# Every fourth slot of two expert passes summed by VectorE in SBUF instead of TensorE in PSUM

## The chip, the cores and the metric

The kernel runs on one core of a Trainium2 chip. The metric is the device time of one execution in microseconds (us); the median of three runs is given, and one further execution was recorded by the hardware profiler.

## The reference, cut to what matters

The reference is a network of three blocks over 256 tokens of width 1024, all in fp32. The last two blocks each end in a PEER layer, a mixture of single-neuron experts. For every token 8 heads choose 16 of 16384 experts each, so 128 experts per token, and

```
h   = sum_d x[t, d] * u[expert, d]          # one dot product per token and expert
a   = gelu(h) * gate
out = sum over the 128 experts of a * v[expert, :]
x   = layer_norm(ALPHA * x + out)
```

`u` and `v` are tables of 16384 rows of 1024 numbers. The rows that are chosen differ from token to token, so they have to be gathered from memory: 8 KB (`u` row and `v` row) per token and expert.

## The kernel before, in words

**Passes and slots.** The 256 tokens are two tiles of 128 (one token per SBUF partition). The two PEER layers and the two tiles make four passes (`PASSES`: layer 0 tile 0, layer 0 tile 1, layer 1 tile 0, layer 1 tile 1), which I number 0 to 3. A pass has 128 slots; slot n (0 to 511 over all passes) handles one expert of each of the 128 tokens of a tile. What the kernel calls the second and third pass are passes 1 and 2, slots 128 to 383.

**One slot.** POOL (GpSimd) waits until a gather buffer is free, then issues an indirect DMA (L2254) that brings 128 rows of 8 KB, 1 MB in all, into one of six buffers (`gbuf`, `GBUF = 6`, used in turn). DVE (VectorE) waits for the landing and computes the dot product with one instruction over 128x1024 (`dot`, L2544) into one column of `hdot`. ACT (ScalarE) applies gelu to that column (L2082), makes a 128x128 diagonal of the gates (L2076, `gate_diagonal`, one slot ahead) and multiplies it by the column (L2089, `diag`, five buffers). PE (TensorE) multiplies this diagonal by the `v` half of the buffer, in two halves of 512 columns, and adds into two PSUM banks which hold the pass's sum (`add_slot`, L1456). The second half's instruction raises `buffer_free`, for which POOL waits six slots later (`wait_freed`).

**What runs beside it.** Slots are only the beat. Four tables (`pe_steps`, `act_steps`, `dve_steps`, and `routing_parts` within the last) say which other work is done ahead of which slot's work on each engine; each engine runs its list strictly in order. In pass 0 that is the queries, keys and routing of the two tiles of layer 0. In passes 1 and 2 it is the whole of the second block for one tile each: keys and values, queries, six dilated-attention units, memory attention, output product, layer norm, and then the PEER queries (16 blocks, `peer_q`, at 96 to 132 slots after the pass's start) and keys. The routing on DVE (top 16 by repeated max, index and one-hot steps) falls into slots 107 to 180 counted from the pass's start, so its later part lies in the next pass. ACT and DVE do their share of a step `LATER = 3` slots or more after PE's. At three slots into the next pass DVE closes the pass before (`add_to_x`, L2547: x = ALPHA*x + sum from PSUM, then statistics) and three slots later normalises (`layer_norm`, L2364).

**Weights.** SP streams weight slots of 128x1024 fp32, in pairs of 1 MB, through a ring of eight slots (L1677) as PE gives them back. The sequence for passes 1 and 2 is laid down in `weight_slots` (`layer`, 44 slots for each of the two tiles). The 16 query blocks of the last PEER layer are partly kept in SBUF: `KEPT` names the even-numbered ones, eight blocks that are loaded once and used in both passes; the other eight go through the ring twice. Four kept blocks have a place of their own, four lie in the arena at columns 0 to 4095.

**Kept loads.** POOL loads the first four kept blocks early, three more after the intra-chunk part of the gated attention of the second block (L2222 to L2224), and the last, which lies at arena column 0, after the last output of that attention has been computed (L2238), just before the first gather. The POOL queue is in order, so the head weights of the first two PEER heads (L2231) come between.

Of the kernel before, what the change touches and what calls it, by code (L numbers as in the profile page):

```python
# [13 lines left out]
ALU = mybir.AluOpType  # L14
ACT = mybir.ActivationFunctionType
AX = mybir.AxisListType.X

P = 128
# [6 lines left out]
PAIR = 2  # L25
KEPT = tuple(range(0, 16, 2))
NEG = -1e30
# [121 lines left out]
def add(table, slot, name, *what):  # L149

    table.setdefault(slot, []).append((name, what))


# [348 lines left out]
def weight_slots(a):  # L502
# [53 lines left out]
    out += [np.zeros((P, SLOT), np.float32)] * (len(out) % PAIR)  # L556
    out += [last_q[i] for i in KEPT]
    out += peer_q[:4] + slots_of_columns(bw[:, 2304:]) + slots_of_rows(a["w_out_2"][1])[NK - 2:]
# [69 lines left out]
def build(nc, x_in, memT_in, weights, consts, where, rows_in, peer_uv, out):  # L628
# [5 lines left out]
    with ctx:  # L634
# [15 lines left out]
        rows = sb("row_ring", [P, NROW, D])  # L650
        kept_apart = sb("kept_queries", [P, len(KEPT) // 2, SLOT])
        cst = sb("const_tile", [P, n_const])
# [142 lines left out]

        kept_queries = [kept_apart[:, i, :] for i in range(4)] + [area(SLOT * i, SLOT) for i in (1, 2, 3, 0)]
        gbuf = [area(4 * SLOT + 2 * D * b, 2, D) for b in GATHER_PLACES]
# [101 lines left out]
        def _(pe):  # L899
# [550 lines left out]
            def add_slot(n):  # L1450

                pe.wait_ge(sem("diag_ready"), n + 1)
                for h in range(2):
# [240 lines left out]
        def _(act):  # L1694
# [383 lines left out]
            def weighted(n):  # L2078

                s = n % P  # L2080
                act.wait_ge(sem("dotted"), n + 1)
                done(act.activation(hdot[:, s:s + 1], hdot[:, s:s + 1], ACT.Gelu), "peer_gelu")  # L2082
                if n + 1 < SLOTS:
                    gate_diagonal(n + 1)
                if n >= DIAGS:
                    wait_freed(act, n - DIAGS)
                act.wait_ge(sem("gate_diag"), n + 1)
                act.wait_ge(sem("peer_gelu"), n + 1)
                done(act.activation(diag[n % DIAGS], gate_diag[n % 2], ACT.Copy, scale=hdot[:, s:s + 1]), "diag_ready")  # L2089
# [98 lines left out]
        def _(pool):  # L2188
# [30 lines left out]
            for r in range(NROW, SPREAD):  # L2219
                if r == NROW + 3:  # L2220
                    wait_drained(pool, ("gla_intra", 0))
                    pool.dma_start(kept_w, weights[n_slots - 2, :, :]).then_inc(sem("kept_loaded"), 16)  # L2222
                    for i in range(4, len(KEPT) - 1):
                        load_kept(i)  # L2224
                pool.wait_ge(sem("rows_used"), r - NROW + 1)
                load_row(pool, r)
                if r == 7:
# [7 lines left out]
                    for i, m in enumerate((mem_k, mem_v)):  # L2235
                        pool.dma_start(kept_out[1][i], last[:, 1024 + 512 * i:1536 + 512 * i]).then_inc(sem("kept_out_loaded"), 16)
            wait_filled(pool, ("gla_o", 3))
            load_kept(len(KEPT) - 1)  # L2238
            for n in range(SLOTS):
# [11 lines left out]
                if n >= GBUF:  # L2251
                    wait_freed(pool, n - GBUF)
                pool.sem_inc(sem("gather_turn"), 1)
                pool.indirect_dma_start(gbuf[n % GBUF].rearrange("p a d -> p (a d)"), None, peer_uv,  # L2254
# [4 lines left out]
        def _(dve):  # L2259
# [279 lines left out]
            def dot(n):  # L2539
# [4 lines left out]
                dve.scalar_tensor_tensor(u, u, 1.0, x[:, t, :], ALU.mult, ALU.mult, accum_out=hdot[:, s:s + 1])\  # L2544
                    .then_inc(sem("dotted"), 1)

            def add_to_x(stage_name, t):  # L2547
# [465 lines left out]
            for n in range(SLOTS + 2 * LATER + 1):  # L3013
                for name, what in DVE_STEPS.get(n, []):
# [14 lines left out]
                    if name == "close":  # L3029
                        p, = what  # L3030
                        if p < len(PASSES) - 1:
                            add_to_x(f"sum{p}", PASSES[p][1])
# [25 lines left out]
                    if name == "out_norm":  # L3058
                        layer_norm(3 + 2 * what[0], what[0], 8, 9, "x_ready")
                if n < SLOTS:  # L3060
                    dot(n)


# [33 lines left out]
```

## Time and profile before

| | |
|---|---|
| median of 3 runs | 2069.1 us (2067.74 to 2071.44) |
| the profiled execution | 2072.72 us |
| its span, first to last instruction | 2070.9 us |
| PE busy | 1895.9 us, 92% of the span |
| DVE busy | 1382.5 us, 67% |
| ACT busy | 896.6 us, 43% |
| POOL busy | 616.1 us, 30% |
| DMA | 708.06 MB, mean 342 GB/s |
| first gather issued, last gather issued | 627.0 us, 2049.8 us |

Busy time is the union of an engine's instructions; idle time is attributed to the instruction that ended it. GB/s counts the bytes of all DMA packets that started in a stretch. The four passes, by the start of their first dot product, begin at 638, 985, 1361 and 1739 us; the last dot product starts at 2059.7 us.

### The profile page before, as it was taken

The page shows a single profiled execution, that of the slowest core. Times are in us where ns is not written, and L with a number is a line of the kernel's source. Part 1 is how long each engine was busy: PE and PEld are TensorE (multiplying, and loading weights), DVE is VectorE, ACT ScalarE, POOL GpSimd, SP SyncE. Part 2 cuts the span into 40 slices and gives each one's busy share as a digit, 9 for nine tenths or more (in the row PEclk, how much of TensorE's full clock was granted, in tenths as well). Part 3 has the DMA queues.
Part 4 walks back from the last instruction along what each step waited for, and adds up shares of the span by engine and source line. Part 5 has one row for each costly group of instructions (what it writes and reads, how often), then busy time and mean ns, then how long its engine had stood idle before and what let it go on. Part 6 is the DMA issues. An engine that isn't in the chain of part 4 may idle for free. (4 is left out here: it accounts for less than half of the span.)

```text
span 2070.9 us, 24820 instructions
## 1 busy us (share of the span) xinstructions
PE 1895.9 (92%) x8012; PEld 1169.3 (56%) x8012; DVE 1382.5 (67%) x2957; ACT 896.6 (43%) x2417; POOL 616.1 (30%) x567
## 2 busy tenths in 40 slices
PE   8999999999998999988899998999999899877776
PEld 8788668887955654433456544556664355322222
DVE  8778666666738677776665545766865575985444
ACT  5657454444534333333334533343455334343332
POOL 0002200000003344444333334443334434444442
PEclk9999999999999999999999999999999999999999
DMA  6623555554658999999999999999999999999997
GB/s 253 224 108 123 194 184 192 193 183 152 235 186 354 390 421 419 418 418 414 400 421 421 421 419 410 417 422 421 417 414 391 416 416 387 422 421 419 421 419 317
DMA packets 99373, 708.06 MB, mean 342 GB/s; under 512 B 11040, under 2 KB 11184, under 8 KB 14896
## 3 DMA queue, kind: packets, MB, share of 16 engines
q0 software_dynamic: 77504, 552.25, 65.1%
q1 hardware_dynamic: 21600, 154.15, 19.8%
q8 instruction: 64, 1.05, 0.2%
q14 instruction: 61, 0.50, 0.1%
q10 hardware_dynamic: 144, 0.11, 0.0%
HBM read 705.42 MB, written 1.05 MB: 341 GB/s over the span
## 5 line engine op out<-in xcount | busy, mean ns | idle before, releaser
L1456 PE MATMUL bank<-arena 128*128 128x512 f32 x2048 | 980.6, 609 | 145.4 <-ACT arena L2089 142.1
L2544 DVE SCALAR_TENSOR_TENSOR arena<-arena,x_tok 128x1024 f32<-128x1024 f32 x512 | 627.1, 1226 | 466.7 <-DMA arena<-peer_uv,arena 461.1
L2254 POOL DMA_INDIRECT arena<-peer_uv,arena x512 | 580.9, 1135 | 850.1 <-PE bank L1456 649.4
L1456 PEld LDWEIGHTS bank<-arena 128*128 128x128 f32 x2048 | 362.0, 191 | 639.4 <-ACT arena L2089 339.7
L2082 ACT ACTIVATE arena<-arena 128x1 f32<-128x1 f32 x512 | 103.6, 202 | 841.7 <-DVE arena L2544 837.7
L2089 ACT ACTIVATE arena<-arena 128x128 f32<-128x128 f32 x512 | 197.7, 386 | 0.5
L2076 ACT ACTIVATE arena<-const_tile,arena 128x128 f32<-128x128 f32 x512 | 197.8, 386 | 0.0
L925 PEld LDWEIGHTS bank<-xT,weight_ring 128*128 128x128 f32 x1248 | 165.5, 191 | 37.0 <-issue 31.1
L925 PE MATMUL bank<-xT,weight_ring 128*128 128x128 f32 (+1 forms) x1248 | 177.2, 294 | 0.9 <-DVE xT L2281 0.9
L925 PE MATMUL bank<-x_low_high,z_high 128*128 128x512 f32 (+1 forms) x480 | 135.8, 351 | 1.5 <-issue 1.5
L1201 PE MATMUL bank<-x_split,w_split 128*128 128x512 f32 x704 | 129.0, 342 | 2.6 <-DVE x_split L2824 2.6
L1201 PEld LDWEIGHTS bank<-x_split,w_split 128*128 128x128 f32 x704 | 110.4, 190 | 20.0 <-issue 2.8
L2806 DVE TENSOR_TENSOR w_split<-weight_ring,w_split 128x1024 fp32r<-128x1024 f32 x66 | 80.8, 1225 | 36.9 <-ACT w_split L1917 36.2
L925 PE MATMUL bank<-x_low_high,ring_low 128*128 128x256 f32 x368 | 104.0, 283 | 0.0
L925 PEld LDWEIGHTS bank<-x_low_high,z_high 128*128 128x128 f32 x480 | 83.5, 190 | 17.1 <-issue 5.2
L871 POOL DMA_DIRECT2D row_ring<-rows_in x8 | 4.5, 571 | 286.6 <-DVEq L2354 200.4
L1917 ACT ACTIVATE w_split<-weight_ring 128x1024 fp32r<-128x1024 f32 x66 | 69.7, 1060 | 42.7 <-PE bank L1201 26.6
L1704 ACT ACTIVATE arena<-bank 128x512 f32<-128x512 f32 (+6 forms) x143 | 67.7, 498 | 45.0 <-PE bank L925 38.1
L925 PE MATMUL bank<-arena 128*64 128x128 f32 (+10 forms) x664 | 74.7, 311 | 2.5 <-DVE arena L2304 1.8
L925 PEld LDWEIGHTS bank<-x_low_high,ring_low 128*128 128x128 f32 x368 | 70.5, 192 | 0.0
L925 PEld LDWEIGHTS bank<-arena 64*128 64x128 f32 (+6 forms) x664 | 54.4, 169 | 28.1 <-issue 23.6
L1767 ACT ACTIVATE z_high<-weight_ring 128x1024 fp32r<-128x1024 f32 x50 | 51.8, 1053 | 34.3 <-PE bank L925 25.5
(322 smaller groups left out, 2035.7 us busy)
## 6 DMA issues: line engine op xcount, KB each, us to landing
weight_ring<-weights SPq DMA_DIRECT2D x145, 1024.0 KB
arena<-peer_uv,arena POOLq DMA_INDIRECT x512
arena<-weights POOLq DMA_DIRECT2D x9, 512.0 KB, 7.9
row_ring<-rows_in POOLq DMA_DIRECT2D x8, 512.0 KB, 4.7
kept_queries<-weights POOLq DMA_DIRECT2D x4, 512.0 KB, 9.8
const_tile<-consts POOLq DMA_DIRECT2D x1, 1657.0 KB, 8.9
x_tok<-x_in SPq DMA_DIRECT2D x2, 512.0 KB, 4.9
memT<-memT_in POOLq DMA_DIRECT2D x1, 1024.0 KB, 7.5
```

Of the source, the lines that this page charges most:

```text
L925: ins = pe.matmul(o, lhsT, rhs, start=start, stop=stop, is_transpose=turn or None)
L1201: ins = pe.matmul(o, lhsT, rhs, start=start, stop=stop)
L1456: ins = pe.matmul(b[:, :], diag[n % DIAGS], gbuf[n % GBUF][:, 1, h * 512:(h + 1) * 512], start=n % P == 0, stop=n % P == P - 1)
L1704: done(act.activation(o, i, f, **kw), "drained_by_act" if last else "act_step")
L1767: done(act.activation(z_high[:, i % SPLITS, :], ring[:, slot % RING, :], ACT.Copy, scale=scale), "z_high")
L1917: done(act.activation(w_split[n % SPLITS][:, 0, :], ring[:, slot % RING, :], ACT.Copy), "slot_high")
L2076: done(act.activation(gate_diag[n % 2], ident, ACT.Copy, scale=w[:, s:s + 1]), "gate_diag")
L2082: done(act.activation(hdot[:, s:s + 1], hdot[:, s:s + 1], ACT.Gelu), "peer_gelu")
L2089: done(act.activation(diag[n % DIAGS], gate_diag[n % 2], ACT.Copy, scale=hdot[:, s:s + 1]), "diag_ready")
L2254: pool.indirect_dma_start(gbuf[n % GBUF].rearrange("p a d -> p (a d)"), None, peer_uv, bass.IndirectOffsetOnAxis(ap=expert[t][:, s:s + 1]. ...
L2544: dve.scalar_tensor_tensor(u, u, 1.0, x[:, t, :], ALU.mult, ALU.mult, accum_out=hdot[:, s:s + 1])\
L2806: done(dve.tensor_tensor(w[:, 1, :], ring[:, slot % RING, :], w[:, 0, :], ALU.subtract), name)
```

## The change

In passes 1 and 2, from the eighth slot of the pass on, every slot with n % 4 == 2 (30 per pass, 60 in all) is not summed by PE. DVE adds `hdot * v` into an SBUF tile `summed` (128x1024, arena column 0) with one instruction, right behind the dot product of the next slot, and frees the buffer itself. For these slots ACT makes no diagonals; it multiplies the 128x1 gelu column by the gate column in place. The pass's close adds `ALPHA * x` to `summed` and then the PSUM halves. `summed` is cleared once per pass. Its place was that of the eighth kept query block, so seven are kept (0, 2, ..., 12), block 14 goes through the ring in both passes, and kept blocks 4 to 6 are loaded behind the head weights.

```diff
-KEPT = tuple(range(0, 16, 2))
+KEPT = tuple(range(0, 14, 2))
...
+def by_dve(n):
+    return P <= n < 3 * P and n % P >= 8 and n % 4 == 2
+
+def gate_no(n):
+    return sum(not by_dve(i) for i in range(n + 1))
...
-    out += [last_q[i] for i in KEPT]
+    out += [last_q[i] for i in KEPT] + [np.zeros((P, SLOT), np.float32)] * (len(KEPT) % PAIR)
...
+        summed = area(0, SLOT)
...
             def add_slot(n):                                   # PE
+                if by_dve(n):
+                    return
...
             def weighted(n):                                   # ACT
...
-                if n + 1 < SLOTS:
+                if n + 1 < SLOTS and not by_dve(n + 1):
                     gate_diagonal(n + 1)
+                if by_dve(n):
+                    w = gate_w[slot_of(n)[1]].rearrange("p h k -> p (h k)")
+                    act.wait_ge(sem("peer_gelu"), n + 1)
+                    done(act.activation(hdot[:, s:s + 1], hdot[:, s:s + 1], ACT.Copy, scale=w[:, s:s + 1]), "diag_ready")
+                    return
...
-                act.wait_ge(sem("gate_diag"), n + 1)
+                act.wait_ge(sem("gate_diag"), gate_no(n))
...
                     pool.dma_start(kept_w, weights[n_slots - 2, :, :]).then_inc(sem("kept_loaded"), 16)
-                    for i in range(4, len(KEPT) - 1):
-                        load_kept(i)
...
-            wait_filled(pool, ("gla_o", 3))
-            load_kept(len(KEPT) - 1)
+            for i in range(4, min(len(KEPT), 7)):
+                load_kept(i)
...
+            def add_slot(n):                                   # DVE
+                s = n % P
+                if n % P > 10:
+                    wait_freed(dve, n - 4)
+                dve.wait_ge(sem("diag_ready"), n + 1)
+                dve.scalar_tensor_tensor(summed, gbuf[n % GBUF][:, 1, :], hdot[:, s:s + 1], summed, ALU.mult, ALU.add)\
+                    .then_inc(sem(f"buffer_free{n % GBUF}"), 1)
+
+            def add_summed(p):
+                t = PASSES[p][1]
+                wait_freed(dve, P * (p + 1) - 2)
+                step(dve.scalar_tensor_tensor(summed, x[:, t, :], ALPHA, summed, ALU.mult, ALU.add))
+                for h in range(2):
+                    cols = slice(h * 512, (h + 1) * 512)
+                    wait_filled(dve, (f"sum{p}", h))
+                    done(dve.tensor_tensor(x[:, t, cols], summed[:, cols], bank((f"sum{p}", h))[:, :], ALU.add), "drained_by_dve")
+                settle()
+                statistics(t)
...
-                        if p < len(PASSES) - 1:
+                        if p in (1, 2):
+                            add_summed(p)
+                        elif p < len(PASSES) - 1:
                             add_to_x(f"sum{p}", PASSES[p][1])
...
+                if n in (P + LATER + 4, 2 * P + LATER + 4):
+                    step(dve.memset(summed, 0.0))
                 if n < SLOTS:
                     dot(n)
+                if by_dve(n - 1):
+                    add_slot(n - 1)
```

## Rows read from the trace of the kernel before

**Rows 1.** The page, part 2: 40 slices of 51.8 us.
```profile
DMA  6623555554658999999999999999999999999997
GB/s 253 224 108 123 194 184 192 193 183 152 235 186 354 390 421 419 418 418 414 400 421 421 421 419 410 417 422 421 417 414 391 416 416 387 422 421 419 421 419 317
```

**Rows 2.** Windows: stretch, length, busy us (x) of PE, PEld, DVE, ACT, POOL, clock, DMA.
```profile
638.00:985.00 347.00, 309.38 (x931) 159.94 (x930) 252.34 (x657) 136.77 (x443) 146.96 (x129) 0.99 1.01 414
985.00:1361.00 376.00, 347.21 (x1383) 198.57 (x1382) 228.08 (x515) 151.94 (x463) 143.84 (x129) 0.99 1.01 416
1361.00:1739.00 378.00, 359.33 (x1510) 215.12 (x1509) 248.36 (x586) 160.07 (x473) 146.94 (x128) 1.00 1.01 411
1739.00:2060.00 321.00, 258.06 (x579) 94.99 (x578) 207.40 (x461) 112.99 (x397) 138.54 (x125) 1.00 1.00 415
...
1900.00:1950.00 50.00, 39.95 (x82) 13.69 (x81) 24.95 (x41) 15.72 (x60) 20.75 (x21) 1.00 1.01 422
```

**Rows 3.** Timeline of bare slots in pass 0: start us, duration us, engine, line.
```profile
981.27 0.20 ACT L2082 ACTIVATE arena<-arena 128x1 f32<-128x1 f32 x1 [1.69 <-DVE arena L2544]
...
981.67 0.39 ACT L2089 ACTIVATE arena<-arena 128x128 f32<-128x128 f32 x1
982.11 1.98 PE L1456 MATMUL bank<-arena 128*128 128x512 f32 x4 [0.49 <-ACT arena L2089]
982.49 1.23 DVE L2544 SCALAR_TENSOR_TENSOR arena<-arena,x_tok 128x1024 f32<-128x1024 f32 x1 [1.26 <-DMA arena<-peer_uv,arena]
982.74 1.79 POOL L2254 DMA_INDIRECT arena<-peer_uv,arena  x1 [1.87 <-issue]
...
984.91 0.94 POOL L2254 DMA_INDIRECT arena<-peer_uv,arena  x1 [0.39 <-issue]
```

**Rows 4.** The page, part 6: DMA issues of SP for the weight ring.
```profile
weight_ring<-weights SPq DMA_DIRECT2D x145, 1024.0 KB
```

**Rows 5.** Windows of stretches in passes 1 to 3, columns as in rows 2.
```profile
1300.00:1330.00 30.00, 25.95 (x111) 14.78 (x110) 27.70 (x86) 11.75 (x36) 10.32 (x11) 1.00 1.01 421
...
1380.00:1400.00 20.00, 18.41 (x80) 10.97 (x80) 17.71 (x57) 8.12 (x28) 9.39 (x8) 1.00 1.02 422
1470.00:1490.00 20.00, 19.07 (x91) 12.35 (x90) 18.46 (x60) 8.85 (x24) 6.80 (x7) 1.00 1.01 418
...
1520.00:1590.00 70.00, 68.25 (x314) 42.93 (x315) 40.92 (x79) 40.19 (x107) 28.27 (x25) 1.00 0.99 393
...
1680.00:1700.00 20.00, 19.42 (x85) 11.50 (x84) 18.71 (x67) 7.34 (x26) 8.47 (x8) 1.00 1.01 419
1700.00:1730.00 30.00, 30.00 (x143) 19.16 (x143) 19.77 (x37) 13.20 (x40) 12.17 (x12) 1.00 0.99 375
1740.00:1760.00 20.00, 18.93 (x79) 10.90 (x78) 14.50 (x24) 9.86 (x29) 8.93 (x8) 1.00 1.00 390
```

**Rows 6.** Chain of waits: by line in 1696 to 1765 us; one piece, start and length.
```profile
by line: PE bank L1456 56.3%; PE bank L925 28.5%; DMA arena<-peer_uv,arena 14.8%; issue 3.2%; DVE arena L2544 1.8%; POOL arena L2254 1.4%; ACT arena L2089 0.6%; ACT arena L2082 0.3%; ACT arena L2076 0.1%; POOLq L2253 0.0%
...
1646.83 5.15 PE bank L1456 x12
...
2029.93 10.00 DMA arena<-peer_uv,arena
```

**Rows 7.** The first gather alone: POOL's timeline, then windows, columns as in rows 2.
```profile
560.07 1.57 POOL L2211 DMA_DIRECT2D arena<-weights  x3
...
626.98 1.02 POOL L2254 DMA_INDIRECT arena<-peer_uv,arena  x1 [7.22 <-DVE arena L2474]
...
604.00:610.00 6.00, 6.00 (x15) 2.46 (x13) 1.75 (x4) 0.29 (x1) 0.00 (x0) 1.00 0.00 0
...
629.00:631.00 2.00, 2.00 (x6) 0.81 (x5) 1.79 (x8) 0.00 (x0) 0.00 (x0) 1.00 0.87 307
```

**Rows 8.** One line of DVE in 985 to 1739 us: busy us, mean ns, idle before.
```profile
L2369 DVE SCALAR_TENSOR_TENSOR x_tok<-x_tok,arena,row_ring 128x1024 f32<-128x1024 f32 x4 | 5.1, 1284 | 0.1
```

**Rows 9.** Window with a lower granted clock, columns as in rows 2.
```profile
1460.00:1470.00 10.00, 8.03 (x24) 4.36 (x23) 7.02 (x13) 5.58 (x14) 4.06 (x4) 0.83 1.02 422
```

More of the change, by code:

```diff
@@ L650, in build @@
         rows = sb("row_ring", [P, NROW, D])
-        kept_apart = sb("kept_queries", [P, len(KEPT) // 2, SLOT])
+        kept_apart = sb("kept_queries", [P, 4, SLOT])
         cst = sb("const_tile", [P, n_const])
@@ L794, in build @@
         mem_PT = [area(25552 + 512 * b, 4, P) for b in range(2)]
-        kept_queries = [kept_apart[:, i, :] for i in range(4)] + [area(SLOT * i, SLOT) for i in (1, 2, 3, 0)]
+        kept_queries = [kept_apart[:, i, :] for i in range(4)] + [area(SLOT * i, SLOT) for i in (1, 2, 3)]
+        summed = area(0, SLOT)
         gbuf = [area(4 * SLOT + 2 * D * b, 2, D) for b in GATHER_PLACES]
@@ L2252, in _ @@
                     wait_freed(pool, n - GBUF)
+                if n == 2 * P // 4 and len(KEPT) == 8:
+                    load_kept(7)
                 pool.sem_inc(sem("gather_turn"), 1)
```

## The prediction

> **What bounds the kernel now.** I read the page's slices first. From 627 us on, where the gathers begin, the DMA engines stand at 9 in every slice but the last and move 387 to 422 GB/s, with three exceptions at the start [rows 1]. The reader is to see a ceiling: the best slices all end at 421 or 422. The windows of the four passes come next [rows 2]. In 1900:1950, where nothing runs but gathers, the rate is 422 GB/s while PE is busy 40 of 50 us and DVE 25 of 50: neither holds the gathers back. So the transfer of bytes is the bound, and an engine matters only where it keeps the rate under 422. What could be won at most is the shortfall, (422 - rate)/422 of each stretch: pass 1 376 x 6/422 = 5.3 us, pass 2 378 x 11/422 = 9.9 us. PE is busy 347 of 376 us and 359 of 378 us there, and that looks like the bound but is not by itself; a busy PE under a full DMA costs nothing.
>
> Where the shortfall lies [rows 5]: 1520:1590 has 70 x 29/422 = 4.8 us, with PE 68 of 70 us and DVE only 41; 1700:1730 has 30 x 47/422 = 3.3 us, with PE 30 of 30 us; 1740:1760, at the close of pass 2, has 1.5 us. The chain of waits agrees for 1696 to 1765: PE 85%, DVE 2% [rows 6]. In pass 1 the shortfall is scattered and stands mostly at layer norms, where DVE is the cause.
>
> How an engine comes to cost DMA time: there are six buffers. A gather issued under load takes 10.0 us to land [rows 6], of which most is queueing, since a lone one, issued at 626.98, moves at 307 GB/s in 629:631 and so needs about 5 us for its 1 MB [rows 7]. Some 5 us of delay in freeing a buffer are thus swallowed by a shorter queue before the DMA runs dry. In a bare slot the buffer is free about 4.1 us after its landing: dot 1.23, gelu and diagonals 0.2 + 0.39 + 0.39, matmuls 1.98, with the hand-overs [rows 3].
>
> **The change part by part.**
>
> *Bytes.* Sixteen query blocks less seven kept leave nine per pass in the ring instead of eight: two weight slots more, one pair of 1 MB. 145 pairs [rows 4] become 146. At 422 GB/s that is 1.05 MB / 0.422 = 2.5 us, inside the stretch that the DMA bounds, and nothing hides it: **+2.5 us**. The load of the eighth block, which goes away, ran just before the first gather, in a stretch with DMA to spare, and gives nothing back.
>
> *Kept loads moved.* Three loads go from 560 us to behind the head weights, about 594 to 596 us. POOL issues them in 1.57 us [rows 7] and then waits until 627 for the first expert anyway. They need 1.5 MB / 0.42 = 3.7 us of DMA, and 604:610 moves nothing at all, so they are done long before 627. They are queued behind the head loads, so they delay neither these nor (SP issues none until 611) the ring. At 560 they no longer compete with the ring; PE was waiting little there. I take -0.3 us, bounds -1.0 and +0.5.
>
> *PE.* 60 slots less. Their four matmul parts take 1.98 us alone and 5.15 / 3 = 1.72 us in a row [rows 3, 6]: 60 x 1.72 = 103 us of PE less, 52 per pass. That is worth only what it adds to the DMA rate. In 1520:1590 about 24 gathers pass, six of them by DVE: 10.3 us of PE's 68.25 go, leaving 58 of 70. I take 4.0 of the 4.8 us, bounds 0 and 4.8. In 1700:1730 PE loses 3 x 1.72 = 5.2 of 30 us, but DVE comes in with a backlog (next part), so I take 1.5 of 3.3 us. Sum **-5.5 us**.
>
> *ACT.* Two diagonals of 0.39 us become one 128x1 instruction of 0.2 us [rows 3]. ACT is busy 152 and 160 us per pass [rows 2], so nothing changes. The new wait of DVE for ACT: the column of slot n is ready some 0.6 us behind its dot product, and DVE asks for it after the next one, 2.5 us later. Behind the waiting instruction on DVE stand the routing and softmax steps and the next dot. Only where ACT itself is late, waiting for PE, does it hold; with PE unloaded I take 0 and keep +1.
>
> *DVE.* The add reads two 128x1024 tensors and writes one. The nearest rows are L2544 with 1.23 us [rows 3] and L2369 with 1.28 us [rows 8]; I take 1.28. 60 x 1.28 = 77 us, on 228 + 248 us busy in 754 [rows 2]: from 63% to 73%. Harmless on average, not in the peaks where routing and attention meet. Adding 1.28 us for each such slot to the busy time [rows 5]: 1300:1330 27.7 + 4 x 1.28 = 32.8 of 30, over by 2.8; 1470:1490 18.5 + 2.6 = 21.0 of 20, over by 1.0; 1680:1700 18.7 + 2.6 = 21.3 of 20, and it goes on into 1700:1710, together up to 3.3 over; 1380:1400, with the longer close, 17.7 + 2.6 + 1.3 = 21.5 of 20, over by 1.5. What is over becomes a later dot and a later free buffer, against some 5 us of slack of which PE's lag, now shorter, had used a part. Also the buffer of such a slot is no longer held by PE at all: freed two DVE instructions after the next landing, 2.5 + 1.23 + 1.28 = 5.0 us instead of 4.1, less where PE lags. I take +1.0 us for the peaks, bounds 0 and 8.6.
>
> *Closes and clearing.* The two halves from PSUM stay, and one instruction over 128x1024 of 1.28 us [rows 8] comes ahead of them, twice. Dots of the next pass wait behind it. At 1380:1400 the rate is 422, so there is slack; at 1740:1760 there is none (390). The two clears of 128x1024 have no row; by the same 1.28 us each they are 2.6 us of DVE at most, in a slot that has room. I take +1.2 us in all, bounds 0 and 5.
>
> *PE's clock.* In passes 1 and 2 bare stretches now leave PE idle some 3 us behind every fourth slot. In 1460:1470 PE was idle 2 of 10 us and the granted clock was 0.83, so a third of the stretch ran at the lower level of 1.2 GHz; the DMA rate stayed at 422 [rows 9]. Such falls may come more often, but in the bare stretches, where the queue has its 5 us of slack. I take 0, bound +2.
>
> Sum: 2.5 - 0.3 - 5.5 + 1.0 + 1.2 = -1.1 us. The profiled execution took 2072.7 us, of which 2070.9 is the span and 1.8 lies around it; it stands 3.6 us above the median of the runs. The change of -1.1 us is put on the median: 2069.1 - 1.1 = **2068.0 us**. Differences below 0.2%, 4.1 us, cannot be told from no change, so the forecast is no change.
>
> *A rule against it.* A gather's issue on POOL takes 0.94 us, but the one at 982.74, begun while DVE's two-input dot of 982.49 ran, took 1.79 [rows 3]. The Trainium skill (SBUF — State Buffer, section "SBUF: two separate sides") states that DVE instructions of this kind and GpSimd share one port pair, and that the loser blocks until the other has finished. By that rule, with which this row agrees, each of the 60 added instructions is another such holder, and the sum would gain what rival C works out from rows; by the average of the rows, in which POOL idles more than half of the time, it gains nothing, and that is what I take.
>
> **The rivals.**
>
> *A, PE's relief comes through whole (faster).* For: in the shortfalls PE is full and the chain is PE's. Against: 1300:1330 and 1680:1700 show DVE at 92 to 94%. All of the shortfall in 1520:1590 and 1700:1730 goes, 8.1 us, and the DVE terms are nil: 2069.1 + 2.5 - 0.3 - 8.1 = 2063.2 us.
>
> *B, DVE takes PE's place (slower).* Place: the four peaks and the two closes. It decides once a dot starts over 5 us behind its landing. For: DVE is over 100% in each of them by the sums above; in 1700:1730 the rate is already low while the DVE backlog of 1680:1700 is worked off. Against: each lasts only 20 to 30 us. Price: peaks 8.6, closes 1.5 + 1.3, PE's relief only 4.0 since 1700:1730 becomes DVE's: 2069.1 + 2.5 - 0.3 + 8.6 + 2.8 - 4.0 = 2078.7 us in full; with half of the peaks and closes 2073.0. I put it at 2076.
>
> *C, POOL's issue is held by the adds (slower).* At most 1.79 - 0.94 = 0.85 us for each. With slack it costs nothing; in the 120 us of 1520:1590, 1700:1730 and 1740:1760, 10 adds x 0.85 = 8.5 us at the most; with half of it on top of the forecast 2072, and where it also meets the DVE backlog 2074.
>
> *D, the relief is where PE was not the bound.* Then nothing of -5.5 comes and 2069.1 + 2.5 - 0.3 + 2.2 = 2073.5 us: barely slower.
>
> **How the numbers follow.** The forecast of no change 0.47 (its own range 2065 to 2073), A 0.22, B 0.20, C 0.04, D 0.07. Faster by over 0.2% is A: 0.22. Slower by over 0.2% is B, C and D: 0.31. The rest is 0.47. The range runs from A's time to B's value: 2063 to 2076.5; below it is only a wholly hidden pair of weights, above it DVE peaks paid in full.
>
> **What would show it.** 146 ring pairs. PE's busy time down by about 100 us, DVE's up by about 80 us. The rate in 1520:1590 (at that place of pass 2) at 415 or more, not 393: the step for PE. A rate of about 375 still behind 1700, with DVE full: B. Rates under 415 in the places of 1300:1330 and 1470:1490: B too. POOL's mean issue time well above its present one: C. The pass lengths 376 and 378 us should become about 378 and 375. The forecast is wrong if either differs by over 4 us, or if the first gather is not issued within 1 us of 627.

## The result, and the profile after

The changed kernel takes 2080.8 us (median of six runs, 2077.6 to 2084.3); the kernel before took 2069.5 us in the six runs beside them. The ratio is 1.0046, interval 1.0032 to 1.0061: slower by 0.46%, or 9.5 us. (The two medians differ by 11.3 us, which the interval holds too; the ratio is the figure used below.) The forecast was 2068.0 us and no change, with 2076.5 us as the upper end of the range. Both missed it. Of the cases it comes nearest to B, DVE in PE's place (2078.7 us in full), though not by B's own sum, as the last part shows.

In the ratios below, 0.001 is 2.07 us. The profiled execution took 2079.8 us, the span 2078.0 us of it.

The page of the kernel after: span, engines, and the 40 slices, here of 52 us. They answer to [rows 1].

```profile
span 2078.0 us, 24346 instructions
PE 1825.7 (88%) x7772; PEld 1136.3 (55%) x7772; DVE 1458.4 (70%) x3021; ACT 882.0 (42%) x2357; POOL 620.8 (30%) x566
DMA  6633555545549999999999999999999999999997
GB/s 239 223 139 105 203 197 196 185 162 183 203 183 383 407 421 421 421 417 413 413 421 419 407 422 400 395 421 422 420 394 414 397 394 393 416 421 421 421 414 314
```

The reader sees the same ceiling of 421 to 422 GB/s as before. PE's busy time is 1825.7 us, 70 us less, and DVE's 1458.4 us, 76 us more (before: 1895.9 and 1382.5 us). The windows of the four passes answer to [rows 2]; columns as there.

```profile
633.00:980.00 347.00, 310.20 (x936) 160.44 (x936) 252.22 (x659) 137.19 (x443) 148.64 (x128) 0.99 1.01 414
980.00:1359.00 379.00, 310.44 (x1252) 181.21 (x1252) 264.17 (x545) 143.17 (x433) 145.22 (x127) 0.95 1.00 412
1359.00:1745.00 386.00, 328.67 (x1422) 202.53 (x1421) 287.33 (x620) 152.46 (x444) 149.49 (x129) 0.96 1.00 407
1745.00:2066.00 321.00, 255.81 (x552) 92.63 (x550) 208.22 (x461) 112.88 (x397) 138.88 (x124) 0.99 1.00 415
```

Pass 1 is 3 us longer (379 against 376), pass 2 is 8 us longer (386 against 378); the passes that the change leaves alone stand. Worked out as in the prediction, (422 - rate)/422 of each pass, the two lose 9.0 and 13.7 us to rates under 422, 22.7 us together, where before they lost 15.2 us. These 7.5 us more and 2.5 us for the new pair's bytes make 10.0 us: apart from the pair's bytes, the loss is time in which the DMA ran below its ceiling. DVE has 264 and 287 us in them, where it had 228 and 248. Then the ring's row, the added instruction, and the matmuls, which answer to [rows 4] and to PE's rows in [rows 3]:

```profile
weight_ring<-weights SPq DMA_DIRECT2D x146, 1024.0 KB
L2571 DVE SCALAR_TENSOR_TENSOR arena<-arena 128x1024 f32<-128x1024 f32 x60 | 76.8, 1281 | 0.0
L1469 PE MATMUL bank<-arena 128*128 128x512 f32 x1808 | 899.8, 628 | 225.6 <-ACT arena L2107 222.6
```

The add takes 1281 ns, sixty times: 76.8 us, as forecast from [rows 8]. The 146 pairs are there. PE is 70 us less busy and not 103: the rest is the lower clock, by which one matmul now takes 628 ns in the mean and took 609, which over 1808 of them is 34 us (the granted clock over the span is 0.977 and was 0.991). The trace has 16 falls to the lower level in passes 1 and 2, 75 us in all, where before had 3 and 14 us. PE had been idle between slots ahead of them: in the two passes it has 26 pauses of over 2 us, up to 4.8 us, where before it had 2.

The places of [rows 5], moved by the few us by which the passes moved:

```profile
1298.00:1328.00 30.00, 20.85 (x96) 12.53 (x94) 29.21 (x84) 10.19 (x32) 10.63 (x10) 1.00 1.01 416
1380.00:1400.00 20.00, 18.15 (x77) 10.62 (x76) 17.17 (x53) 7.17 (x24) 8.17 (x8) 1.00 1.02 421
1473.00:1493.00 20.00, 17.15 (x96) 12.16 (x95) 18.23 (x59) 7.64 (x19) 6.58 (x7) 1.00 1.01 421
1523.00:1593.00 70.00, 61.68 (x293) 39.37 (x292) 47.30 (x83) 37.29 (x95) 29.16 (x26) 0.98 1.01 412
1687.00:1707.00 20.00, 14.18 (x67) 8.76 (x66) 19.48 (x65) 4.54 (x18) 8.32 (x7) 1.00 0.96 385
1707.00:1737.00 30.00, 26.61 (x125) 16.72 (x124) 23.17 (x40) 13.13 (x40) 12.87 (x13) 1.00 0.96 366
1746.00:1766.00 20.00, 16.36 (x58) 8.77 (x57) 16.32 (x26) 9.97 (x29) 7.49 (x7) 0.91 0.99 402
```

DVE is full in the first (29.2 of 30 us) and the fifth (19.5 of 20), and the rates are 416 (was 421), 385 (419) and 366 (375). 1380:1400 and 1473:1493 keep 421. 1523:1593 rose from 393 to 412, which looked like PE's relief; the experiments do not bear that out. What DVE does ahead of the 366 is in its timeline, with a gather's issue at the end:

```profile
1700.99 1.22 DVE L2562 SCALAR_TENSOR_TENSOR arena<-arena,x_tok 128x1024 f32<-128x1024 f32 x1
1702.14 1.28 DVE L2571 SCALAR_TENSOR_TENSOR arena<-arena 128x1024 f32<-128x1024 f32 x1
1703.34 0.75 DVE L2432 MAX8 arena<-arena 128x8 f32<-128x256 f32 x2
1704.12 1.22 DVE L2562 SCALAR_TENSOR_TENSOR arena<-arena,x_tok 128x1024 f32<-128x1024 f32 x1
1704.23 1.93 POOL L2272 DMA_INDIRECT arena<-peer_uv,arena  x1 [3.11 <-DVE arena L2571]
```

Dot, add, top-8 step and dot follow each other without a gap: here DVE does not wait for a landing, and POOL's gather of 1704.23 has waited 3.11 us for the add L2571 to free its buffer. The chain of waits over 1674 to 1745 us, against [rows 6] where PE had 85% and DVE 2%:

```profile
by line: DMA arena<-peer_uv,arena 42.8%; DVE arena L2562 16.2%; issue 13.1%; PE bank L1469 5.6%; DVE arena L2571 4.1%; DVE arena L2430 2.8%; DVE arena L2434 2.8%; POOL arena L2272 2.7%; DVE arena L2428 2.6%; DVE arena L2432 2.1%; DVE arena 
```

PE's matmuls of the sum are down to 5.6%; the named lines of DVE make 30.6%, and the gathers' flights (from issue to landing) 42.8%.

### The profile page after: what moved, and what is told of

The parts are those of the page before. It is cut to its first block and busy times, and to the rows that moved or that the text cites. A ratio compares the mean times of both kernels' runs of the same rounds, so it can differ in the third digit from the quotient of the medians.

```text
span 2078.0 us, 24346 instructions
## 1 busy us (share of the span) xinstructions
PE 1825.7 (88%) x7772; PEld 1136.3 (55%) x7772; DVE 1458.4 (70%) x3021; ACT 882.0 (42%) x2357; POOL 620.8 (30%) x566
## 5 line engine op out<-in xcount | busy, mean ns | idle before, releaser
L1469 PE MATMUL bank<-arena 128*128 128x512 f32 x1808 | 899.8, 628 | 225.6 <-ACT arena L2107 222.6
L2272 POOL DMA_INDIRECT arena<-peer_uv,arena x512 | 586.2, 1145 | 879.6 <-PE bank L1469 577.8
L1469 PEld LDWEIGHTS bank<-arena 128*128 128x128 f32 x1808 | 325.6, 195 | 688.9 <-ACT arena L2107 424.1
L936 PEld LDWEIGHTS bank<-xT,weight_ring 128*128 128x128 f32 x1280 | 171.1, 194 | 33.7 <-issue 27.2
L936 PE MATMUL bank<-xT,weight_ring 128*128 128x128 f32 (+1 forms) x1280 | 183.5, 297 | 0.8 <-DVE xT L2299 0.8
L2107 ACT ACTIVATE arena<-arena 128x128 f32<-128x128 f32 x452 | 176.5, 390 | 7.5
L2089 ACT ACTIVATE arena<-const_tile,arena 128x128 f32<-128x128 f32 x452 | 175.5, 388 | 0.0
L1930 ACT ACTIVATE w_split<-weight_ring 128x1024 fp32r<-128x1024 f32 x66 | 69.8, 1062 | 42.5 <-PE bank L1212 26.6
L2571 DVE SCALAR_TENSOR_TENSOR arena<-arena 128x1024 f32<-128x1024 f32 x60 | 76.8, 1281 | 0.0
L936 PE MATMUL bank<-weight_ring,arena 128*128 128x512 f32 (+1 forms) x192 | 64.9, 528 | 0.2 <-ACT arena L1717 0.2
```

The source lines that it names most:

```text
L936: ins = pe.matmul(o, lhsT, rhs, start=start, stop=stop, is_transpose=turn or None)
L1469: ins = pe.matmul(b[:, :], diag[n % DIAGS], gbuf[n % GBUF][:, 1, h * 512:(h + 1) * 512], start=n % P == 0, stop=n % P == P - 1)
L1930: done(act.activation(w_split[n % SPLITS][:, 0, :], ring[:, slot % RING, :], ACT.Copy), "slot_high")
L2089: done(act.activation(gate_diag[n % 2], ident, ACT.Copy, scale=w[:, s:s + 1]), "gate_diag")
L2571: dve.scalar_tensor_tensor(summed, gbuf[n % GBUF][:, 1, :], hdot[:, s:s + 1], summed, ALU.mult, ALU.add)\
```

## The experiments

All ratios are to the kernel before, with 95% intervals; they reach 0.1 to 0.15% to either side, so the difference of two ratios is known to 0.15 or 0.2%, 3 to 4 us. The diffs are cut and against the changed kernel, except that of e2. Three kernels form the base: e1 has the bytes without the adds, e3 the bytes and DVE's time without the adds' relief, e4 the relief without DVE's time.

**e1, no adds.** Seven blocks kept, loads moved, no sum by DVE.

```diff
 def by_dve(n):
-    return P <= n < 3 * P and n % P >= 8 and n % 4 == 2
+    return False
...
-                        if p in (1, 2):
-                            add_summed(p)
-                        elif p < len(PASSES) - 1:
+                        if p < len(PASSES) - 1:
...
-                if n in (P + LATER + 4, 2 * P + LATER + 4):
-                    step(dve.memset(summed, 0.0))
```

> All of the change but the sums: seven kept query blocks, block 14 through the ring twice, kept loads 4 to 6 behind the head weights; PE sums every slot as before. Theory 1 (VectorE's peaks, and the lower TensorE clock that its adds leave behind, make the loss): only the bytes remain, 2.5 us, less what the moved loads give (the profile of the changed kernel issued its first gather 4.4 us earlier): 2067 to 2072 us, passes 1 and 2 as long as before plus 2.5 us together. Rival (the extra ring pair costs more than its bytes because PE waits for it): 2075 us or more, with PE waiting for weight_ring in passes 1 and 2.

Measured: 1.0011 [1.0001, 1.0020], 2072.2 us. That is +2.3 us for the pair of 1 MB, where the prediction had 2.5 - 0.3. The interval runs from 0.2 to 4.1 us, and e5 and e8 below, with the same bytes, measured 1.0000; so the size of this term is known to some 2 us only.

**e2, the kernel before with the kept loads moved alone.**

```diff
-                    for i in range(4, len(KEPT) - 1):
-                        load_kept(i)
...
+            for i in range(4, len(KEPT) - 1):
+                load_kept(i)
             wait_filled(pool, ("gla_o", 3))
```

> The kernel before with kept loads 4 to 6 issued behind the head weights and nothing else; eight kept. If the 4.4 us that the changed kernel's profile gained ahead of the first gather come from this step, it reads 2065 us and a first gather at 622 to 623 us. If they are the spread of one profile against another (the change's own forecast was -0.3 us), it reads 2069 us and the first gather stands anywhere from 622 to 628.

Measured: 0.9998 [0.9990, 1.0007]. The move is worth nothing that can be told.

**e3, DVE's time alone.** e1 with the clears and sixty instructions of the add's form, whose result nobody reads.

```diff
-                if by_dve(n - 1):
-                    add_slot(n - 1)
+                if P < n <= 3 * P and (n - 1) % P >= 8 and (n - 1) % 4 == 2:
...
+                    dve.scalar_tensor_tensor(summed, x[:, slot_of(n - 1)[1], :], 1.0, summed, ALU.mult, ALU.add)\
+                        .then_inc(sem("filler"), 1)
```

> e1 with 60 instructions of 128x1024 more on VectorE at the places of the adds, and two clears, which no other engine needs and whose result is not used; PE sums every slot, so its lag and its clock stay those of before. Theory 1a (VectorE's peaks alone): shortfall of the DMA rate rises at the four places of the changed kernel's (slots 112 to 119 of pass 1, 40 to 55, 88 to 95 and 112 to 119 of pass 2) by some 10 us or more, since PE's lag is not relieved: 2080 us or more. Theory 1b (the clock of a PE that idles is the larger part): under 2075 us.

Measured: 1.0045 [1.0029, 1.0060], 2079.1 us. The whole loss is there, with PE doing all 128 slots of a pass: 0.34% or 7.0 us above e1, by the two intervals 3 to 11 us. One of these idle instructions (idle in that they do nothing for the result) took 1223 ns:

```profile
L3108 DVE SCALAR_TENSOR_TENSOR arena<-x_tok,arena 128x1024 f32<-128x1024 f32 x60 | 73.4, 1223 | 0.0
```

**e4, PE's relief alone.** The sixty slots are left out of the sum, ACT frees their buffers, DVE adds nothing; the clears and the longer closes are out too.

```diff
                     done(act.activation(hdot[:, s:s + 1], hdot[:, s:s + 1], ACT.Copy, scale=w[:, s:s + 1]), "diag_ready")
+                    act.sem_inc(sem(f"buffer_free{n % GBUF}"), 1)
                     return
...
-                if by_dve(n - 1):
-                    add_slot(n - 1)
```

> The changed kernel without VectorE's adds, clears and the longer close: the 60 slots are left out of the sum altogether, ScalarE frees their buffers as soon as the gated column is ready. VectorE carries no more than before; PE has the changed kernel's gaps and clock. Theory 1a: PE's relief comes through, 8 us of shortfall go, 2.5 us of bytes come: 2062 to 2066 us in spite of falls of the clock. Theory 1b: the falls of the clock (16 in passes 1 and 2 against 3) eat the relief: 2069 us or more, with shortfall in bare slots 64 to 71 and behind layer norms.

Measured: 1.0008 [0.9998, 1.0018], 2071.6 us: 0.6 us under e1, which the intervals can't tell from nothing; 5.5 us less is outside them. It has 18 falls of the clock.

**e8, the relief given back as useless work.** e4, and for each slot left out PE multiplies zeros into the same banks.

```diff
                 if by_dve(n):
+                    pe.wait_ge(sem("diag_ready"), n + 1)
+                    for h in range(2):
+                        pe.matmul(bank((f"sum{n // P}", h))[:, :], c("eps")[:, 3:4].to_broadcast([P, P]), cst[:, where["keysT"][0]:where["keysT"][1]], start=False, stop=False)
                     return
```

> e4 with two matmuls of a zero column over constants on PE in the place and at the time of each sum left out (they add zero and hold no buffer): 103 us of PE work given back that does nothing. Theory 1b: falls of the clock go from 18 in passes 1 and 2 to 3, and the time is the same as e4's 2071.6 within 1.5 us, since what the idle saves the lower clock takes. Rival (relief in e4 was worth something and something else ate it): 2074 us or more.

Measured: 1.0000 [0.9990, 1.0010]. PE's busy time in the two passes is back (708 us; e1 705, e4 641), its clock falls 3 times as before the change, and the time is the same or less. The 103 us of matmuls have no price that can be told in this kernel, with them or without.

**e11, the same in the change itself.** The zero matmuls of e8 put into the changed kernel.

```diff
                 if by_dve(n):
+                    pe.wait_ge(sem("diag_ready"), n + 1)
+                    for h in range(2):
...
                     return
```

> The changed kernel whole, with e8's two zero matmuls on PE in place of each of the 60 sums: PE has the work and the clock of before, VectorE its adds. Theory (the relief of PE is worth nothing, since the clock takes it): 2079 to 2081 us, no slower than the changed kernel, about 3 falls of the clock in passes 1 and 2. Rival (relief is worth something against VectorE's backlog): 2083 us or more.

Measured: 1.0052 [1.0039, 1.0064], 2081.5 us, against 1.0046 of the change: what PE was relieved of is worth nothing measurable there either. The clock's falls are down to 5 in it (0.991 over the span), so they are not the cause of the loss.

The three places of the trace say the same. First the windows of e1, then of e3 and e4, at 1520:1590, at the end of pass 1, and at the end of pass 2; columns as before.

```profile
1520.00:1590.00 70.00, 68.01 (x315) 42.67 (x314) 41.04 (x80) 39.50 (x103) 28.08 (x25) 1.00 1.00 403
1320.00:1345.00 25.00, 22.82 (x102) 13.76 (x102) 16.95 (x35) 10.85 (x32) 11.03 (x9) 1.00 1.00 411
1695.00:1740.00 45.00, 44.84 (x205) 28.02 (x204) 29.78 (x66) 19.21 (x62) 17.94 (x17) 1.00 1.00 387
```

```profile
1520.00:1590.00 70.00, 69.57 (x327) 44.56 (x327) 50.68 (x96) 42.71 (x106) 27.46 (x24) 1.00 1.01 408
1320.00:1345.00 25.00, 22.07 (x97) 13.05 (x96) 23.20 (x48) 11.53 (x35) 9.02 (x9) 1.00 0.98 390
1695.00:1740.00 45.00, 41.29 (x179) 24.52 (x179) 38.50 (x92) 17.04 (x55) 17.03 (x16) 1.00 0.96 365
```

```profile
1520.00:1590.00 70.00, 60.86 (x275) 37.59 (x274) 40.58 (x79) 37.26 (x95) 23.95 (x24) 0.93 0.97 396
1320.00:1345.00 25.00, 20.12 (x99) 12.98 (x97) 13.57 (x26) 7.60 (x28) 10.37 (x11) 1.00 1.00 402
1695.00:1740.00 45.00, 41.41 (x204) 27.32 (x204) 30.16 (x61) 17.43 (x56) 21.54 (x18) 0.96 0.97 385
```

and of the kernel after and of e8:

```profile
1520.00:1590.00 70.00, 63.26 (x297) 40.03 (x295) 47.97 (x87) 38.97 (x100) 29.27 (x25) 0.98 1.01 411
1320.00:1345.00 25.00, 20.77 (x96) 12.87 (x95) 17.62 (x33) 10.09 (x29) 12.73 (x9) 1.00 0.94 366
1695.00:1740.00 45.00, 38.26 (x186) 24.48 (x185) 36.02 (x73) 17.09 (x54) 18.93 (x17) 1.00 0.95 370
```

```profile
1520.00:1590.00 70.00, 69.78 (x320) 43.47 (x318) 42.16 (x81) 37.52 (x97) 25.93 (x26) 1.00 1.00 411
```

At 1520:1590 the rate does not follow PE: 408 and 411 GB/s with PE at 69.6 and 69.8 of 70 us (e3, e8), 396 with PE at 60.9 (e4). The rise from 393 to 412 was no proof of the relief. (The windows stand at fixed times, and the slots in them shift by up to 6 us from profile to profile, so a few GB/s mean nothing.) At the other two places it goes with DVE: 390 and 365 with DVE at 23.2 of 25 and 38.5 of 45 us (e3), 366 and 370 in the kernel after, but 411 and 387 in e1, and 402 and 385 in e4, whose PE has 3.4 us less in the last. In the kernel after, DVE is busy only 17.6 of 25 us in the first of the two, but 29.2 of 30 us just ahead of it (1298:1328). The shortfall that e1 and the kernel before have in 1695:1740 (387 and 389) stays in e4, so PE's sums do not explain that one either; what does is open.

**e5, e6, e7: a few slots where PE was full.** e5 is e4 with 14 slots of pass 2 left out, 40 to 79 and 112 to 127. e6 has these summed by DVE. e7 has ten, 52 to 79 and 116 to 127, summed by DVE.

```diff
-    return P <= n < 3 * P and n % P >= 8 and n % 4 == 2
+    return (296 <= n < 336 or 368 <= n < 384) and n % 4 == 2
```

> e4 with only 14 of the 60 slots left out of the sum (slots 40 to 79 and 112 to 127 of pass 2, each fourth), where PE is full; buffers freed by ScalarE. Theory 1b (in e4 the falls of the clock ate the relief): few falls are added, the shortfall of pass 2 at slots 56 to 71 and 112 to 127 goes from some 6 us to 2: 2067 to 2069 us, 3 to 5 us under e1. Rival (PE was not what held the rate there): 2072 us, as e1.

> The change with only those 14 slots summed by VectorE; pass 1 closes as before. Theory (loss = VectorE's added time at its peaks, relief real where PE is full): most of the 7 us that VectorE's adds cost are gone, relief of 3 us stays, 1.3 us for the longer close: 2070 to 2072 us. Rival (a VectorE add costs the same wherever it stands): e1 plus 14/60 of 7 us = 2074 us.

> As e6 with the slots that lie in VectorE's two peaks taken out: 10 slots (52 to 79 and 116 to 127 of pass 2). Theory: 1 to 2 us under e6, 2069 to 2071 us, no slower than the kernel before. Rival: no different from e6.

Measured: e5 1.0000 [0.9990, 1.0009], e6 1.0007 [0.9997, 1.0018], e7 1.0011 [1.0000, 1.0021]. None is faster than the kernel before, and all three intervals overlap that of e1: e5 stands 0.11% under e1, which may be relief or nothing, and e6 and e7 can't be told from e5. Three of e7's ten slots (54, 118 and 122) lie in what e9 and e10 below count as DVE's full stretches.

**e9, e10: where DVE's time costs.** The idle instructions of e3, split: e10 has the twenty that fall in DVE's full stretches, e9 the other forty. The stretches are slots 88 to 95 (the layer norms) and 106 to 122 of both passes and 34 to 54 of pass 2.

```diff
+def peak(n):
+    return 216 <= n < 224 or 234 <= n <= 250 or 290 <= n <= 310 or 344 <= n < 352 or 362 <= n <= 378
...
+                loads = [i for i in range(P, 3 * P) if i % P >= 8 and i % 4 == 2 and not peak(i)]
+                if n - 1 in loads:
```

> e3 with 40 of its 60 idle VectorE instructions, those outside the stretches where VectorE is full (taken out: slots 88 to 95 and 106 to 122 of pass 1, 34 to 54, 88 to 95 and 106 to 122 of pass 2; 20 instructions). Theory (VectorE's added time costs only at its peaks): 2072.5 us, within 1.5 us of e1; e3's other 5 to 6 us of the 7 stand in the 20. Rival (each add costs the same): 2/3 of e3's 0.34%, 2077 us.

> The other 20 of e3's 60 instructions alone, those in the full stretches. Theory: 2077 to 2079 us, nearly e3. Rival (each costs the same): 1/3 of 0.34%, 2074.5 us.

Measured: e9 1.0011 [0.9999, 1.0022], nothing above e1. e10 1.0028 [1.0018, 1.0037], 0.17% above e1: a third of the instructions, half of the cost at the middle of the intervals. If each instruction cost the same wherever it stands, e9 would be at 1.0034, outside its interval; e10's own expectation, 2077 to 2079 us, was missed with 2075.8 us. The two together are 0.17% above e1 and e3 is 0.34%. The intervals are too wide to say whether the rest appears only with all sixty.

**e12, e18, e17: the same split with the real adds.** e12 sums the forty off the peaks by DVE, e18 the twenty in them; e17 is e12 with the zero matmuls of e8.

```diff
-    return P <= n < 3 * P and n % P >= 8 and n % 4 == 2
+    return P <= n < 3 * P and n % P >= 8 and n % 4 == 2 and not peak(n)
```

> The changed kernel with VectorE's sums at the 40 slots outside the full stretches only, the other 20 by PE. Theory: e1's 2072 us plus the longer closes, 1 to 2 us: 2073 to 2074 us, 7 us under the changed kernel. It does not beat the kernel before, whose bytes are fewer. Rival (each add costs the same): 2078 us.

> The changed kernel with VectorE's sums at the 20 slots in the full stretches only; PE's idle slots are fewer than in e12, in stretches where PE is full too. Theory (VectorE's time in its peaks costs 0.17% beside e1, and PE's relief there offsets part of it): 1.0015 to 1.0028, 2074 us. Rival (relief of PE is worth nothing and its idle slots cost as in e12): 1.003 or more.

> e12 with the two zero matmuls on PE in place of each of the 40 sums: the same adds, buffers and closes, PE's work and clock as before the change. Theory L (VectorE's work off the peaks costs only together with a PE that idles, whose clock falls): 1.0011 to 1.0018, 2072 to 2074 us, few falls. Rival (a real add costs whatever PE does): as e12, 1.0034, 2077 to 2078 us.

Measured: e12 1.0034 [1.0022, 1.0045], e18 1.0030 [1.0018, 1.0042], e17 1.0032 [1.0020, 1.0045]. e18 agrees with e10. e12 does not agree with e9: it is 0.23% above, and e17 shows that neither PE's idle time nor its clock is why. Nor is it a wait for ACT: the rows of the adds in e12 and e17 have 0.0 us of idle time before them. The theory set down for e12 (2073 to 2074 us) failed, and its rival, each add costs the same (2078 us), has the measured 2077.9; for e18 too the rival's 1.003 or more came. Forty adds cost 0.23% above e1, twenty 0.19%, sixty 0.35%: for the real adds a price per add fits within the intervals, and a price in the peaks alone does not. Windows of e12 and e18 at the two ends of passes:

```profile
1320.00:1345.00 25.00, 23.34 (x96) 13.63 (x96) 15.55 (x30) 10.57 (x32) 11.49 (x10) 1.00 1.01 415
1695.00:1740.00 45.00, 44.83 (x203) 27.85 (x204) 30.31 (x66) 18.14 (x58) 19.16 (x17) 1.00 0.99 389
```

```profile
1320.00:1345.00 25.00, 21.25 (x93) 13.23 (x93) 18.30 (x34) 10.50 (x32) 11.12 (x9) 0.93 0.93 377
1695.00:1740.00 45.00, 39.19 (x189) 25.12 (x188) 34.50 (x69) 17.42 (x56) 19.64 (x17) 1.00 0.96 371
```

The low rates at the peaks go with the adds in them (377 and 371 GB/s in e18, 415 and 389 in e12). What e12 loses lies elsewhere, scattered, and stays open.

The traces of all kernels show the same split in the dots themselves. I counted, over passes 1 and 2, how far a dot starts behind its landing, that is behind the last update of the semaphore for which it waits. It is over 4.5 us behind in five slots of the kernel after, 116 of pass 1 and 113 to 116 of pass 2; in the last four it grows 5.1, 5.2, 6.0, 6.5 us. The eight kernels with DVE's additional work in all of the peaks (the kernel after, e3, e10, e11, e14, e15, e16, e18) have 5 or 6 such slots each, all of them from 111 to 117 of pass 2 and at 115 or 116 of pass 1, with a largest lag of 6.5 to 7.4 us. The other twelve, e9, e12 and e17 among them (and e6 and e7, which have adds in some slots of the peaks), have none; their largest lag is 3.3 to 4.4 us. So the late dots go with the peaks' part of the loss, and they are not what e12 and e17 lose.

**e13, e14: the closes.** e13 is e1 with the change's clears and longer closes. e14 is the changed kernel with the close of before, so that DVE's sum is left out of x.

```diff
-    return P <= n < 3 * P and n % P >= 8 and n % 4 == 2
+    return False
...
-                wait_freed(dve, P * (p + 1) - 2)
```

> e1 with the clears of the sum tile and the longer closes of passes 1 and 2 alone; no slot is summed by VectorE. Theory H (the held buffer is what a real add costs): the closes are worth 1 to 2 us, 1.0011 becomes at most 1.0020, 2072 to 2074.5 us. Rival K (the closes are it): 4 us or more, 1.003 or more.

```diff
-                        if p in (1, 2):
-                            add_summed(p)
-                        elif p < len(PASSES) - 1:
+                        if p < len(PASSES) - 1:
```

> The changed kernel with the closes of before: what VectorE has summed in the 60 slots is left out of x. Theory H: 1 to 2 us under the changed kernel, 2079 us, 1.004. Rival K: 4 us or more under it, 1.0025 or less.

Measured: e13 1.0008 [0.9996, 1.0020], e14 1.0059 [1.0042, 1.0075]. The longer close costs nothing that can be told where it is added and gives nothing where it is taken away.

**e15, the buffers freed early.** e4 with the clears and the sixty idle instructions: DVE's time as in the change, but ACT frees the buffers.

```diff
+                if by_dve(n - 1):
+                    dve.wait_ge(sem("filler"), sum(by_dve(i) for i in range(n - 1)))
+                    dve.scalar_tensor_tensor(summed, x[:, slot_of(n - 1)[1], :], 1.0, summed, ALU.mult, ALU.add)\
+                        .then_inc(sem("filler"), 1)
```

> e4 (60 slots left out of the sum, buffers freed by ScalarE) with e3's 60 idle instructions on VectorE and its two clears: the changed kernel's load on VectorE and relief of PE, but no buffer waits for VectorE's add, and the closes of before. Theory H: 3 us or more under the changed kernel, 1.003 or less, about 2076 us. Rival (what costs is VectorE's time, the buffer does not matter): as e3, 1.0045.

Measured: 1.0046 [1.0029, 1.0062], the same as e3 and as the change. That the add itself holds a buffer costs nothing measurable; DVE's time is enough for the whole loss.

**e16, the add ahead of the next dot.**

```diff
-                if n < SLOTS:
-                    dot(n)
                 if by_dve(n - 1):
                     add_slot(n - 1)
+                if n < SLOTS:
+                    dot(n)
```

> The changed kernel with VectorE's add of slot n - 1 ahead of the dot product of slot n instead of behind it: the buffer is free one dot product (1.2 us) and the wait for the landing sooner, the next dot product and all that needs it up to 1.3 us later. Theory H: faster than the changed kernel by 1 to 3 us, 2078 to 2080 us. Rival (the dot products set the pace, and VectorE now waits for ScalarE's column with the dots behind it): 2083 us or more.

Measured: 1.0055 [1.0040, 1.0070], 2080.8 us, between theory and rival. The order does not mend it.

## Why the prediction was wrong

*Bytes, +2.5 us, and the moved loads, -0.3 us:* right as far as can be told. 146 pairs, +2.3 us (e1), 0 (e2). The first gather is issued at 622.6 us and not within 1 us of 627. The kernels with the moved loads have it between 621 and 626 us and the one profile of the kernel before at 627; but e2, with the moved loads, is not faster, so a first gather some 4 us earlier did not show in the time.

*PE, -5.5 us:* wrong, measured -0.6 us (e4 against e1), and nothing that can be told by e8 and e11. The step that failed is "PE 68 of 70 us and DVE only 41", read as cause. The prediction itself had said that "a busy PE under a full DMA costs nothing", and then credited PE with 4.0 of the 4.8 us because it was the busiest engine of a stretch with a low rate. e8 keeps PE as busy there and has 411 GB/s. What holds the kernel before at 393 is not shown; e1, with the ring's pairs one place on, had 403 to 405.

*DVE's peaks, +1.0 us:* wrong, and the larger of the two misses. DVE's time costs 7.0 us (e3 against e1), inside the bounds of 0 and 8.6 and close to the upper one, which is the plain sum of what is over 100%. The count of 77 us was right. That the 7.0 lies so near 8.6 is in part luck: the sum holds the peaks alone, and of the real adds the twenty in the peaks cost 3.9 us above e1 (e18) and the forty outside them 4.8 us (e12). I took 1.0 because each peak is short and each late buffer has some 5 us of slack. But lateness is carried from slot to slot: the lag behind the landing grows from 5.1 to 6.5 us over four slots of pass 2, up to 7.4 us in e3, and was at most 3.3 us before. That is B's point, "over 5 us behind its landing", and it is reached behind one of the four peaks, 1680:1700 (dots at 1708 to 1717 us), and nearly (4.9 us) at slot 116 of pass 1, just behind 1300:1330. The other two held: 1380:1400 and 1473:1493 are at 421 GB/s, and 1298:1328 itself fell to 416 only. The layer norms at slots 88 to 95, which were not named, lost 1.4 us of DMA time in pass 1 and 0.7 in pass 2 before and 2.4 and 3.1 after (bytes of the packets between landings, at 422 GB/s, against the time); but e1 without adds has 3.0 and 1.6 there and e8 1.5 and 3.1, so this rise is not shown to be the adds'.

*ACT's wait, 0; the clock, 0:* right as far as the runs tell. The row of L2571 has 0.0 us of idle time before the adds, the idle instructions of e3 don't wait for ACT and cost the same as the adds, and the zero work of e11 takes most of the falls of the clock away without a gain. *Closes and clears, +1.2 us:* not told from 0 in e13 and e14.

*C, POOL's issue:* not seen. A gather's issue takes 1145 ns in the mean, before 1135; the median is 940 ns, before 939. First the row of the kernel before, then that of the kernel after:

```profile
L2254 POOL DMA_INDIRECT arena<-peer_uv,arena x512 | 580.9, 1135 | 850.1 <-PE bank L1456 649.4
L2272 POOL DMA_INDIRECT arena<-peer_uv,arena x512 | 586.2, 1145 | 879.6 <-PE bank L1469 577.8
```

The kernels without DVE's additional work have means from 1103 (e8) to 1144 ns (e2), and e3 with it has 1135, so 10 ns are nothing. The gather of 1704.23 above took 1.93 us beside a dot of DVE; the one of 982.74 before took 1.79. The Trainium skill (SBUF — State Buffer, section "SBUF: two separate sides") lets the loser of the shared port wait. These two rows agree; in the means nothing of it is seen, on an engine that is idle 70% of the time.

*The signs.* PE's busy time is down by 70 us and not 100, for the clock's reason given above; DVE's is up by 76. 1523:1593 has 412 GB/s, under the 415 that was to show PE's step, and at this place e3 and e8 have 408 and 411 without relief. Behind 1700 the rate is 366 after a full DVE, as B has it; at 1298:1328 and 1473:1493 it is 416 and 421, which B has under 415. Pass 2 takes 386 us and not 375, which by the prediction's own words makes it wrong.

The ledger: 0.11% bytes, 0.34% DVE's time, nothing measurable for all else, 0.45% together; the change costs 0.46%. The near agreement is better than the intervals of the parts allow one to claim. With these sizes the prediction's sum would have been 2069.5 + 2.3 + 7.0 = 2078.8 us, within the interval. Its range went wrong by the same two steps: D and B were held apart (2073.5 and 2076), though both came about together. B's full price of 2078.7 us is close by luck: its peaks of 8.6 and closes of 2.8 (1.5 of 1380:1400 stands in both), less 4.0 of relief, make 7.4 us, where the runs have 7.0, nothing and 0.6.

One profile of each kernel bears out that it is DVE's time. Over passes 1 and 2, the time lost to rates under 422 GB/s, from the bytes of all packets, is 14.3 to 19.1 us in the seven kernels in which DVE has no additional instructions but at most the clears and closes (before, e1, e2, e4, e5, e8, e13), and 19.5 to 28.3 us in the six with sixty (e3, e11, e14, e15, e16, after).

*Still open:* why forty real adds off the peaks cost 0.2% (e12, e17) and forty idle instructions there cost nothing (e9), when all sixty cost the same in either form (e3, e15, the change). The intervals of e9 and e12 just touch, so part of it may be spread. That DVE's time is the cost is shown; that it costs in its peaks is shown for a part of it only. No version was faster than the kernel before.

## What to carry to other kernels

Work that is moved to another engine costs time of the engine that receives it, though its mean load (here 72% over the two passes) leaves room. Sum what goes over 100% in its busiest stretches, do not let each piece draw on the same slack again, and keep a price for the rest: here forty adds outside those stretches were not free either. The engine that is relieved gave back nothing here, and its high busy share in a stretch with a low DMA rate did not show that it held the rate down. Give the relieved engine zero work in place of the old before the relief is counted; one kernel settles it.

## What the runs showed that was not expected

103 us of matmuls can be left out, or replaced by zeros, with 1.0008 and 1.0000: in 754 us in which PE was busy 94% of the time, these matmuls had no price that can be told. Nor had the lower clock: with PE's longer pauses the granted clock fell to the lower level 16 times in the change and 18 times in e4 instead of 3, and was 0.75 over these 20 us of the kernel after:

```profile
1635.00:1655.00 20.00, 15.01 (x31) 5.59 (x29) 15.62 (x25) 8.84 (x26) 9.30 (x8) 0.75 0.93 357
```

Kernels with the falls (e4, the change) and with few (e8, e11: 3 and 5) do not differ by more than the intervals; nor do e15 (15 falls, 1.0046) and e3 (4, 1.0045). In this one stretch the rate was 357 GB/s, so a fall can coincide with a loss, but in the whole it adds up to nothing that can be told.
